# Where the split weights of each chunk start inside their SBUF buffers

## The reference

```
z = h @ w_in                                  # 1024 x 5320, first layer
y = (gates * (branch outputs @ w_branch)) @ w_out
(gelu(conv(a)) * g) @ w_down                  # a, g = h @ w_up: 1024 x 5632; w_down: 2816 x 1024
proj = x @ gla_w_in;   y = (...) @ gla_w_out  # second layer, chunked linear attention
kv = x @ w_kv;  q = x @ swa_w_in;  y = (...) @ swa_w_out   # third layer, dilated attention
```

## The kernel before, in words

| buffer | whi0, whi1, whi2 | wlo0, wlo1, wlo2 | hhi, hlo | uhi, ulo | gohi, golo, wgo | yhi, ylo | ohi, olo |
|---|---|---|---|---|---|---|---|
| before | 0, 0, 0 | 0, 0, 0 | 64, 64 | 64, 64 | 64, 64, 64 | 0, 0 | 32, 32 |

## Time and profile before

### The profile page before, as it was taken

The page is one execution under the profiler, slowest core; times in us unless marked ns, Lnnn a source line. Parts: engine busy times, 40 slices in busy tenths (PEclk is TensorE's granted clock), DMA queues, the critical chain, the costliest instruction groups (busy, mean ns, idle before and its releaser), DMA issues.

```text
span 749.9 us, 14222 instructions
## 1 busy us (share of the span) xinstructions
PE 723.9 (97%) x5964; PEld 703.3 (94%) x5964; DVE 524.3 (70%) x778; ACT 395.7 (53%) x560; POOL 104.4 (14%) x87
## 2 busy tenths in 40 slices
PE   8999999998899999999999999999999999999995
PEld 6799899897898999999999989899999999999995
DVE  4979878886978687778776657836576356555665
ACT  4297455555354545544544348537554465556551
POOL 0030000000521000000000130000004465443000
PEclk9999999999999999999999999889999999999999
DMA  8995576566364456565567453604446654333101
GB/s 345 411 361 177 216 278 245 190 240 225 113 225 169 143 195 210 188 221 164 205 267 275 165 199 129 210 25 170 169 155 225 204 191 131 126 138 113 57 1 57
DMA packets 22265, 141.13 MB, mean 188 GB/s; under 512 B 2389, under 2 KB 3029, under 8 KB 6458
## 3 DMA queue, kind: packets, MB, share of 16 engines
q1 hardware_dynamic: 21626, 137.28, 50.4%
q0 software_dynamic: 576, 2.95, 1.0%
HBM read 139.17 MB, written 1.05 MB: 187 GB/s over the span
## 4 chain that ended last, share of the span: by engine, by line
PE 71%; DVE 13%; issue 7%; ACT 6%; DMA 2%; POOL 1%; DVEq 0%; ACTq 0%; POOLq 0%
PE res L1631 22%; PE res L1596 12%; PE res L1598 12%; PE res L1597 12%; ACT whi L639 4%; DVE wlo L1052 3%; PE pX L1816 2%; PE pX L1995 2%; PE pS L1796 1%; DMA shared<-in_w_ada 1%; DVE raw L1065 1%; PE pS L1657 1%; ACT sq L654 1%; DVE shared L1065 1%; PE pT L1806 1%
## 5 line engine op out<-in xcount | busy, mean ns | idle before, releaser
L1052 DVE TENSOR_TENSOR wlo<-raw,whi 128x2048 fp32r<-128x2048 f32 (+3 forms) x101 | 226.9, 2250 | 119.2 <-ACT whi L639 112.7
L639 ACT ACTIVATE whi<-raw 128x2048 fp32r<-128x2048 f32 (+3 forms) x101 | 188.2, 1865 | 102.0 <-issue 73.3
L1596 PE MATMUL res<-hhi,whi 128*128 128x256 f32 (+1 forms) x576 | 166.1, 288 | 4.1 <-DVE wlo L1052 1.5
L1597 PE MATMUL res<-hhi,wlo 128*128 128x256 f32 (+1 forms) x576 | 161.0, 280 | 0.0
L1598 PE MATMUL res<-hlo,whi 128*128 128x256 f32 (+1 forms) x576 | 161.0, 279 | 0.0
L1596 PEld LDWEIGHTS res<-hhi,whi 128*128 128x128 f32 (+1 forms) x576 | 107.5, 187 | 5.9 <-issue 3.4
L1597 PEld LDWEIGHTS res<-hhi,wlo 128*128 128x128 f32 (+1 forms) x576 | 107.5, 187 | 0.3
L1598 PEld LDWEIGHTS res<-hlo,whi 128*128 128x128 f32 (+1 forms) x576 | 107.2, 186 | 0.2
L1631 PE MATMUL res<-hhi,whi 128*128 128x256 f32 x544 | 106.8, 278 | 0.0
L1631 PE MATMUL res<-hlo,whi 128*128 128x256 f32 x544 | 106.4, 277 | 0.0
L1631 PE MATMUL res<-hhi,wlo 128*128 128x256 f32 x544 | 106.3, 277 | 0.0
(11 more groups left out here) (340 smaller groups left out, 1344.4 us busy)
## 6 DMA issues: line engine op xcount, KB each, us to landing
raw<-in_wts SPq DMA_DIRECT2D x97, 1024.0 KB, 4.9
raw<-in_w_ada SPq DMA_DIRECT2D x16, 1024.0 KB, 5.2
shared<-in_w_ada SPq DMA_DIRECT2D x6, 1024.0 KB, 11.0
gates<-in_wts SPq DMA_DIRECT2D x4, 768.0 KB, 13.1
raw<-in_wts SPq DMA_DIRECT2D x4, 768.0 KB, 6.0
y<-in_w_ada SPq DMA_DIRECT2D x2, 1024.0 KB, 9.3
x<-in_xT SPq DMA_DIRECT2D x2, 512.0 KB, 4.5
gv<-in_ln_rows POOLq DMA_DIRECT2D x1, 1024.0 KB, 7.4
```

The costliest lines, as they stand in the source:

```text
L639: nc.scalar.activation(hi[:, 0:kt * w], raw[RAW_OF["w", c] % RAW][:, 0:kt * w], ACT.Copy).then_inc(hi_ready, 1)
L1052: nc.vector.tensor_tensor(lo[:, 0:b], raw[RAW_OF["w", c] % RAW][:, 0:b], hi[:, 0:b].bitcast(f32), ALU.subtract).then_inc(lo_ready, 1)
L1596: mm(out, ah, bh, start=first, stop=False)
L1597: mm(out, al, bh, start=False, stop=False)
```

## The change

Every weight buffer becomes 24 float32 (96 bytes) longer, and `halves(c)` returns, for all chunks but 79 and 105, a view that begins 4 times (`c` modulo 7) float32 further, 0, 16, 32, ... 96 bytes. Both halves of a chunk are shifted alike, and writers and readers get the same view.

```
+SHIFT = [4 * (c % 7) for c in range(NC)]

-        whi = [sb(f"whi{i}", [P, CW], f32r) for i in range(SPL)]
-        wlo = [sb(f"wlo{i}", [P, CW], f32r) for i in range(SPL)]
+        whi = [sb(f"whi{i}", [P, CW + 24], f32r) for i in range(SPL)]
+        wlo = [sb(f"wlo{i}", [P, CW + 24], f32r) for i in range(SPL)]
...
-            return whi[c % SPL], wlo[c % SPL]
+            return tuple(h[c % SPL][:, SHIFT[c]:SHIFT[c] + CW] for h in (whi, wlo))
```

## The result

| | us |
|---|---|
| the kernel before, median of 20 runs beside the change | 757.66 (751.16 to 761.21) |
| the changed kernel, median of 20 runs | 760.90 (758.69 to 762.11) |
| ratio | 1.0058, interval 1.0034 to 1.0081 |
| profiled span, before and after | 749.9 and 759.0 |
| predicted | 765, range 745 to 777 |

The change costs 0.6%, clear of noise and less than 1%. The two profiled spans differ by more, 9.1 us. The runs of the kernel before stand in two groups, and that accounts for it. Nine of the 20 are at 751.2 to 754.8 us, eleven at 757.0 to 761.2, and the profiled execution of before (751.74) belongs to the lower one. The changed kernel has one group, 758.7 to 762.1 us, where the upper group of before is.

A forecast was written before the change was run, and what follows sets the result against it. The time was taken as TensorE's instruction count times their pitch. Terms of +10.2, +2.4 and -0.5 us gave +12.1 us, 763.8 against the profiled 751.7 or 766.0 on the median; forecast 765, range 745 to 777.

The forecast's parts named there:

- within 1%: Whole kernel at 746.3 to 761.4 us: rival A plus the lower end of the forecast's own case; chance 0.30.
- the favoured one: Whole kernel slower by over 1%, as the relation sets the pitch and most relations are worse than 64; chance 0.55.
- TensorE's reads are the term that counts: Class 64 falls from 4440 to 712 matmuls; longer buffers and splits cost 0, splits at most 2.5 us.
- The relation of the starts sets the pitch: TensorE's fp32r matmuls: stationary minus moving start modulo 128, with a lasting state, sets 113.3, 117.8 or 120.0 ns.
- rival A: Pitch is no matter of addresses; 120 ns belongs to stages, the output projections; 753.9 us, 749 to 757; chance 0.20.
- The prices by class: Per matmul: 0 and 32 at 120.0 ns, 96 at 119.2, 64 at 115.5, 16/112 at 119.8, 48/80 at 117; mean 118.6.
- The predicted pattern in chunk number: Pitch differs by chunk with a pattern modulo 21 (3 buffers by 7 shifts), lowest where both halves are near 64.
- Term 1: Stretches at 113.3 ns with TensorE full: 1923 matmuls, each 5.3 ns dearer, +10.2 us, nothing hiding it.
- Terms 2 and 3: Other 2517 of class 64: 1.6 ns dearer each, 60% counted, +2.4 us; the 414 at about 120 ns: -0.5 us.
- From the profile to the median: 763.8 us from the profiled 751.7, or 766.0 with that execution's 2.1 us below the median; 765 chosen between.
- B: Changing relations disturb the slow state, so 113.3 ns in all of it; 742 us, 738 at the lower bound; chance 0.15.
- C: Starts off 32 bytes cost a further piece, up to 126.7 ns for 2079 matmuls; +27 us, 781 us; chance 0.10.

The follow-up runs named there:

- all_at_64: Changed kernel's longer buffers, but one constant shift per weight buffer, bringing stationary minus moving back to 64 modulo 128; 748.26 us, ratio 0.9895 to the kernel before.
- pads_only: Changed kernel with its buffers 96 bytes longer but no chunk shifted; 759.99 us, ratio 1.0080 to the kernel before.
- relation_64_of_256: Kernel before with weights in two gapless tensors, both halves shifted by a constant 128 bytes; nine runs, median 749.21 us, ratio 0.9914.
- off_by_4_bytes: Kernel before with weights in two gapless tensors, both halves shifted by one float32; 763.00 us, ratio 1.0081.
- no_turned: Kernel before without the two calls of turned, six matmuls whose results nobody reads; 758.48 us, ratio 1.0032.

## Why the prediction was right, and where it was off

The direction, the place and the mechanism (TensorE's reads, by the relation of the starts) were right; the prices inside it and the size on the median were not. The measured 760.9 us lies 4.1 us under the forecast of 765: 3.0 us because the profiled spans differ by 9.1 and not by 12.1, and some 1.2 us from the placing above 763.8. Against the kernel before it is 0.6% slower, so it fell into the case "within 1%" that had 0.30, and not into the favoured one.

- **TensorE's reads are the term that counts, the rest costs nothing.** Held: the splits' medians moved by 5 and 1 ns, the wait for `wlo` by 0.1 us.
- **The relation of the starts sets the pitch.** Held. The prediction had it from three stretches that also differed in loop and stage, which rival A used. `all_at_64` against `pads_only`, which differ in nothing but the starts of the weights inside their buffers, makes 11.7 us between the medians.
- **The prices by class.** The mean came out at 118.17 ns for 118.6 predicted, but with the wrong inside, so its closeness is partly luck. I had a slope, cheap near 64 and dear near 0. In the changed kernel the feature-major pitches have these means by class, 0 to 112: 118.1, 118.6, 118.6, 117.9, 117.7, 118.0, 118.2, 118.5 ns. The class 64, for which I took 115.5, is hardly cheaper than the others, and the dear ones are under 120. What goes with it in every chunk is a partner half that is off 64. The predicted pattern in chunk number is there, but it goes by the pair of relations and isn't lowest near 64: in `w_up` the chunks take from 116.9 ns (halves at 80 and 112) to 119.5 (48 and 80), and of the eight chunks of L1632 that stand 42 further on, with the same buffers and shifts, seven repeat their pitch within 0.3 ns. 120.0 ns, read from `wgo` and `ohi`, belongs to some loops and was no price for a class.
- **Term 1, 1923 matmuls by 5.3 ns, +10.2 us.** About right in the profiles: 4.70 us on the 960, 0.42 us on the 96, and 1424 instead of 1485 matmuls in 168 us is 4.85 ns each, 9.3 us for 1923.
- **Terms 2 and 3, +2.4 and -0.5 us.** About right as pitch. Matched one by one in the two traces, the other matmuls of the class 64 went from a mean of 117.05 ns (I had 117.0) to 118.15, +2.7 us, and the 414 gained 0.4 us. With 9.2 us for term 1 the pitches add up to 11.5 us of the 12.1 predicted. The span grew by 9.1 only. Of the difference, 0.9 us is the small float32 matmuls `pX` (L1995 before, L1996 after), 11.45 us before and 10.55 after: the granted clock was partly at its lower level there, 1.2 GHz, and in the mean 0.56 from 479 to 492 us before and 0.64 from 487 to 500 us after. The rest are shorter gaps at other places. In the two further profiles of the kernel before that row takes 11.38 and 10.23 us, so it varies without the change.
- **From the profile to the median: the step that failed.** "That execution is 2.1 us below the median of the runs" was treated as an offset between measurements, and the sum was added on top. It is a difference between two groups of runs, most likely of pitch mode. Of 93 runs of the kernel before in all comparisons here, 51 are at 748.8 to 754.8 us and 42 at 756.4 to 761.2. I priced the loss of something as if every run had it, and part of the runs seem not to. Against the median of the lower group of the first comparison (753.57) the changed kernel is 7.3 us slower, against that of the upper (759.95) 1 us, and the mixture gives 0.6%. The three runs known then, 751.5, 753.9 and 757.0, lie on both sides of the gap; their spread of 0.7% for one program was the hint.
- **The rivals.** A fell with `all_at_64`. B, that variety helps, was wrong for this change, where the variety leaves the class 64. Within that class something like it came true: the kernels with halves 128 bytes apart, `all_at_64` and `relation_64_of_256`, are faster than the one with a constant relation. C's further cost was not found in any whole kernel, the highest mean pitch being 118.6 ns; beyond 121 ns are only single groups, such as the `ohi` products of `off_by_4_bytes`.
- **The page of the Trainium skill** (SBUF — State Buffer, "SBUF: two separate sides") says that TensorE never waits on anyone for SBUF. Read as "addresses are free", as the prediction did for its sum of 0, it doesn't agree with the runs, and the measurement decides: in `w_up` other starts inside the same buffers take the pitch from 113.6 ns (`all_at_64`, its slow first chunk included) to 118.3 (`pads_only`). Whether TensorE waits there, no run shows.

**What stays open.** Why 64, and what the mode physically is, no run tells. Nor was the exact width of the class 64 measured: the runs 4 and 16 bytes off it also have the halves 128 bytes apart modulo 256, with the high one at 196 and 208, and the pair 192 and 64 was never run feature-major. That the upper group of the kernel before is executions with `w_up` or other long stretches on the plateau is argued, not shown: none of its three profiles fell into that group. `no_turned` shows only that such a mode at these addresses costs 4.3 us on the 960 matmuls. For it speaks the size: some 1490 matmuls of `w_up` and `w_down` by 4.5 ns are 6.7 us (an estimate from these traces), and the medians of the two groups are 752.7 and 759.2 us. And why two loads of three at 64 keep more in `w_down` than in `w_up` wasn't looked into.

## What to carry to other kernels

Where TensorE is never idle and still has room, compare the pitch of equal matmuls across stages; a busy share of 100% hid 4% here. Then try the relation between the two operands' starts, with a constant shift of a buffer, in steps that keep everything else, and read the relations of all operands, modulo more than the step in mind, from the built program: a gapless layout moved one half by 128 bytes here unnoticed, and the two kernels with the gain are those with such halves at 64 modulo 128. The best of the versions here, the two tensors with a 128 byte shift or the six constants of `all_at_64`, are 0.9 and 1.1% faster than the kernel before (ratios 0.9914 and 0.9895) and, by their medians, 1.5 and 1.7% faster than the changed one, with the same instructions. And before a sum is put on top of a median, look whether the runs of the kernel before are one group.

## What the runs showed of the hardware

- fp32r matmuls, 256 columns moving, 128 loaded, both from SBUF: 113.3 ns in long stretches only where stationary minus moving start is 64 bytes modulo 128 for all loads of a product and the mode has been entered. In `w_up` it is 117.8 ns at 64 without the mode (`no_turned`) and 117.8 to 118.5 elsewhere (80 and 0, each held constant modulo 128; mixtures). Other loops have 119 to 120 ns at 0 and 32.
- Off 64 the pitch of a chunk goes with the pair of relations of its halves: 118.0, 119.4 and 117.7 ns in turn in `pads_only`.
- The mode lasts over more than a thousand matmuls (some 1490 in a row before, from 251.0 to 419.5 us) and is switched by other matmuls in between: the three of `turned` begin the fast pitch at 192 modulo 256 (113.1 us for 960 matmuls without them, 108.8 with), and end it in `all_at_64`.
- With both halves at the same relation modulo 256, 64 or 192, whole chunks occur in either mode. Feature-major, with the high half at 64 and the low at 192, all 175 chunks of three profiles but one (116.2 ns) take 113.3 to 115.1 ns past the first dozen matmuls; token-major, at 192 and 64, 26 chunks of two profiles take 116.9 to 117.9 ns.
- The same program can have a stretch in either mode from one execution to the next: 192 matmuls in 22.61 us in two executions, 168 in 18.95 in another.
- The two splits hardly show where their operands start: ScalarE's copy has a median of 1909 to 1914 ns in the profiles with all starts at multiples of 32 bytes and 1914 to 1916 in the three others, VectorE's subtraction 2291 to 2293 and 2292 to 2294.
